# All 31 taps of the second mixer stage's convolution in four 64x64 tiles of TensorE

## What is computed

```python
def conformer_conv(a, b, w_dw, b_dw, ln_g, ln_b):
    u = a * jax.nn.sigmoid(b)
    y = lax.conv_general_dilated(          # causal, depthwise, 31 taps
        u, w_dw[:, None, :], window_strides=(1,), padding=[(CONV_KERNEL - 1, 0)],
        dimension_numbers=('NWC', 'WIO', 'NWC'), feature_group_count=CONV_WIDTH)
    y = layernorm(y + b_dw, ln_g, ln_b)
    return jax.nn.silu(y)

y_conv = conformer_conv(...)               # 512 channels
y_nsa = nsa_mixer(...)                     # 8 heads of 64
h = h + jnp.concatenate([y_conv, y_nsa], axis=-1) @ w_out[l]
```

## Time and profile before

| | us |
|---|---|
| median of 3 runs | 1631.72 (1630.59 to 1637.64) |
| span of the profiled execution | 1634.1 |
| TensorE busy | 1572.9 (96%) |
| VectorE busy | 1188.7 (73%) |
| ScalarE busy | 861.1 (53%) |
| GpSimd busy | 351.8 (22%) |

### The profile page before, as it was taken

The page is one execution under the profiler, slowest core; times in us unless marked ns, Lnnn a source line. Parts: engine busy times, 40 slices in busy tenths (PEclk is TensorE's granted clock), DMA queues, the critical chain, the costliest instruction groups (busy, mean ns, idle before and its releaser), DMA issues.

```text
span 1634.1 us, 31405 instructions
## 1 busy us (share of the span) xinstructions
PE 1572.9 (96%) x10490; PEld 1437.0 (88%) x10490; DVE 1188.7 (73%) x2258; ACT 861.1 (53%) x1587; POOL 351.8 (22%) x260
## 2 busy tenths in 40 slices
PE   8899998999999999999999999999999999999997
PEld 8789987999887887898999999988888999999996
DVE  3788676788756678455579678779998767776776
ACT  5564445655556643565554555554444545444544
POOL 2344332011000422122048755540000000000000
PEclk9899999999999999999999999999999999999999
DMA  7333244555564720154546644457777665555654
GB/s 268 126 103 104 91 142 155 171 162 180 188 194 126 234 76 1 42 191 142 168 150 203 201 149 145 136 184 241 241 241 227 201 183 190 182 190 183 189 186 148
DMA packets 87848, 271.15 MB, mean 166 GB/s; under 512 B 9824, under 2 KB 26336, under 8 KB 87392
## 3 DMA queue, kind: packets, MB, share of 16 engines
q1 hardware_dynamic: 65088, 237.01, 45.2%
q10 hardware_dynamic: 22688, 33.16, 6.2%
HBM read 258.60 MB, written 11.53 MB: 165 GB/s over the span
## 4 chain that ended last, share of the span: by engine, by line
PE 80%; DVE 11%; ACT 4%; issue 2%; POOL 1%; ACTq 1%; DMA 0%; DVEq 0%; POOLq 0%
PE ps_chunk L488 42%; PE ps_misc L488 21%; PE ps_misc L295 7%; PE ps_chunk L295 4%; PE ps_misc L2457 4%; DVE ffn_arena L1584 1%; DVE w_lo L428 1%; ACT w_hi L421 1%; PE ps_misc L798 1%; DVE mixers_arena L2257 1%; DVE mixers_arena L2258 1%; DVE mixers_arena L2254 1%; PE ps_chunk L495 1%; POOL w_lo L428 1%; DVE mixers_arena L2253 1%
## 5 line engine op out<-in xcount | busy, mean ns | idle before, releaser
L421 ACT ACTIVATE w_hi<-raw 128x512 fp32r<-128x512 f32 (+1 forms) x900 | 548.5, 626 | 495.2 <-PE ps_chunk L488 292.0
L428 DVE TENSOR_TENSOR w_lo<-raw,w_hi 128x512 fp32r<-128x512 f32 x671 | 490.1, 745 | 269.1 <-ACT w_hi L421 259.4
L488 PE MATMUL ps_chunk<-x_hi,w_hi 128*128 128x256 f32 x1792 | 520.0, 290 | 13.6 <-DVE w_lo L428 7.3
L488 PE MATMUL ps_chunk<-x_hi,w_lo 128*128 128x256 f32 x1792 | 508.6, 284 | 0.0
L488 PE MATMUL ps_chunk<-x_lo,w_hi 128*128 128x256 f32 x1792 | 508.3, 284 | 0.0
L428 POOL TENSOR_TENSOR w_lo<-raw,w_hi 128x512 fp32r<-128x512 f32 (+2 forms) x229 | 299.8, 1323 | 539.3 <-ACT w_hi L421 476.0
L488 PEld LDWEIGHTS ps_chunk<-x_hi,w_hi 128*128 128x128 f32 x1792 | 344.8, 192 | 26.1 <-POOL w_lo L428 10.2
L488 PEld LDWEIGHTS ps_chunk<-x_hi,w_lo 128*128 128x128 f32 x1792 | 345.0, 193 | 3.2 <-issue 0.5
L488 PEld LDWEIGHTS ps_chunk<-x_lo,w_hi 128*128 128x128 f32 x1792 | 344.8, 192 | 0.0
L488 PE MATMUL ps_misc<-w_hi,hid_hi 128*128 128x512 f32 x520 | 203.5, 391 | 2.1 <-DVE hid_lo L2536 1.4
L488 PE MATMUL ps_misc<-w_hi,hid_lo 128*128 128x512 f32 x520 | 203.1, 391 | 0.0
(11 more groups left out here) (342 smaller groups left out, 1795.4 us busy)
## 6 DMA issues: line engine op xcount, KB each, us to landing
raw<-in_stream SPq DMA_DIRECT2D x452, 512.0 KB, 3.6
early_rows<-row ACTq DMA_DIRECT2D x64, 128.0 KB, 1.7
row<-early_rows ACTq DMA_DIRECT2D x62, 128.0 KB, 3.2
memory_kv<-mixers_arena ACTq DMA_DIRECT2D x4, 512.0 KB, 5.2
mixers_arena<-in_cmp_w ACTq DMA_DIRECT2D x1, 2048.0 KB, 7.7
mixers_arena<-memory_kv ACTq DMA_DIRECT2D x4, 512.0 KB, 6.3
mixers_arena<-in_consts ACTq DMA_DIRECT2D x1, 1729.0 KB, 7.9
row<-in_rows ACTq DMA_DIRECT2D x3, 512.0 KB, 6.6
```

What stands on the lines that cost most here:

```text
L421: e.activation(w_hi[q % 2][:, s], raw[q][:, s], ACT.Copy).then_inc(made, 1)
L428: e.tensor_tensor(w_lo[q % 2][:, s], raw[q][:, s], w_hi[q % 2][:, s].bitcast(F32), ALU.subtract).then_inc(made, 1)
L488: last = e.matmul(o, stationary[a], moving[b], start=start and i == 0, stop=stop and i == 2, skip_group_check=True)
```

## The change

All 31 taps become products. The 128x128 diagonal of a channel tile holds two 64x64 diagonals, and the other two quarters of the array stand idle; now two channel tiles are worked on at once. For each tap and pair of tiles there are four 64x64 products: rows 0 to 63 and 64 to 127 of the first tile, summed in the same half of PSUM's partitions, and both halves of the second, summed in the other half (`rows ^ swap`). The row half chooses the bank. The diagonals are built by GpSimd in four parts of 8, 8, 8 and 7 taps per pair, with a folded identity `eye`. The taps strand, its sums in ps_chunk[0] and the four adds of L1865 are gone; instead VectorE moves each tile out of PSUM in two halves of 64 partitions, with the bias. The order string is another one: the letters t are gone and some letters c stand elsewhere.

```diff
--- before.py
+++ after.py
@@ -42,7 +42,7 @@
 NF = D_FF // P
 
 CONV_K, CONV_T = 31, 4
-CONV_PE = 20
+CONV_PART = 8
 NSA_H, NSA_G, NSA_D = 8, 2, 64
 CMP_B, CMP_S = 32, 16
 N_CMP = (T - CMP_B) // CMP_S + 1
@@ -73,9 +73,8 @@
 LAST_QUARTER_LAST = ((0, 0), (0, 1), (1, 0), (1, 1), (0, 2), (1, 2), (0, 3), (1, 3))
 
 MIXERS_2_ORDER = ("ddqddddddkddqqddddddddddddddkdddddddddkdddddddqddddddqdddddqqddkddqdqkkkkddqdkdkdddkkccddkdddddddkkk"
-                  "ddccttddkdkkqtqdkdddqqkcctttccttkkctttktctttkqqcttkkqtcccttqtttttttqqttkktctttttctttkttttqtttckttqkq"
-                  "tttttttttttttttckccctccttcccctqcckqckcckqccqkccqckckqckcccqqccqkqkccqccccckqccccqkcqckqkqdddqqkkdddd"
-                  "dddddddddddddddddddddddddddddddddddddddddckqt")
+                  "ddccddkdkkqqdkdddqqkcccckkckckqqckkqcccqqqkkcckqckqkqckcccccccccqcckqckcckqccqkccqckckqckcccqqccqkqk"
+                  "ccqccccckqccccqkcqckqkqdddqqkkdddddddddddddddddddddddddddddddddddddddddddddckq")
 
 STREAM = {}
 _at = 0
@@ -1812,9 +1811,9 @@
                 return have_2, have_cmp
 
             keys, queries = nsa(Z2, first, causal, seen, seen_add, inv, pos_raw, cmpw1, cmpw2, begin, x_parts)
-            conv, taps = conv_module(Z2, first, x_parts)
+            conv = conv_module(Z2, first, x_parts)
             weave(MIXERS_2_ORDER, dense=(0, 4, dense_chunks()), conv=(2, 2, conv), keys=(4, 2, keys()),
-                  queries=(6, 2, queries()), taps=(0, 2, taps))
+                  queries=(6, 2, queries()))
             return added_by["w_out_2"]
 
         def conv_module(Z2, first, x_parts):
@@ -1823,24 +1822,31 @@
             pad = CONV_K - 1
             U = cut(CONV_T, T + pad)
             Y = cut(CONV_T, T)
-            half = CONV_PE // 2
-            diagonals = [cut(half, P), cut(half, P)]
+            part_of_taps, side = [range(j, min(j + CONV_PART, CONV_K)) for j in range(0, CONV_K, CONV_PART)], P // 2
+            block = [slice(0, side), slice(side, P)]
+            diagonals = [cut(2, CONV_PART, side), cut(2, CONV_PART, side)]
+            eye = cut(side)
             tiles = lambda n: Z2[:, n, :].rearrange("p (k t) -> p k t", t=T)
             taps = col[:, COLS["conv_dw_w_2"][0]:COLS["conv_dw_w_2"][0] + CONV_K * CONV_T].rearrange(
                 "p (j k) -> p k j", k=CONV_T)
-            made, summed = [], [None] * CONV_T
-            sums_at = ps_chunk[0][:, :].rearrange("p (k t) -> p k t", t=T)
+            made = []
 
             def taps_by_pe():
                 used_up = [None, None]
 
-                def diagonal_taps(k, part):
-                    D_part, lo = diagonals[part], half * part
+                jobs = [(pair, part) for pair in range(CONV_T // 2) for part in part_of_taps]
+
+                def diagonal_taps(n):
+                    pair, part = jobs[n]
+                    count = len(part)
+                    each = taps[:, 2 * pair:2 * pair + 2, part[0]:part[0] + count]
                     return pool.do(lambda e: e.tensor_tensor(
-                        D_part, ident.unsqueeze(1).broadcast_to([P, half, P]),
-                        taps[:, k, lo:lo + half].unsqueeze(2).broadcast_to([P, half, P]), ALU.mult), used_up[part])
+                        diagonals[n % 2][:, :, 0:count, :],
+                        eye.unsqueeze(1).unsqueeze(1).broadcast_to([P, 2, count, side]),
+                        each.unsqueeze(3).broadcast_to([P, 2, count, side]), ALU.mult), used_up[n % 2])
                 yield from evacuated(first)
-                m = [diagonal_taps(0, 0), diagonal_taps(0, 1)]
+                pool.do(lambda e: e.tensor_tensor(eye, ident[:, 0:side], ident[:, side:P], ALU.add))
+                m = [diagonal_taps(0), diagonal_taps(1)]
                 dve.do(lambda e: e.memset(U[:, :, 0:pad], 0.0))
                 yield
                 for b, ready in enumerate((half_evacuated, evacuated)):
@@ -1848,49 +1854,33 @@
                     made.append(dve.do(lambda e, s=slice(2 * b, 2 * b + 2): e.tensor_tensor(
                         U[:, s, pad:pad + T], tiles(3)[:, s, :], tiles(4)[:, s, :], ALU.mult)))
                     yield
-                for k in range(CONV_T):
-                    at, ps, free = banks.take()
-                    for part in range(2):
-                        for some in range(0, half, 2):
-                            for j in range(half * part + some, half * part + some + 2):
-                                used_up[part] = pe.do(mm(ps[:, 0:T], diagonals[part][:, j - half * part, :],
-                                                         U[:, k, j:j + T], j == 0, j == CONV_PE - 1),
-                                                      m[part], made[k // 2], *free)
+                for n, (pair, part) in enumerate(jobs):
+                    if part[0] == 0:
+                        at, ps, free = banks.take(2)
+                    for j in part:
+                        for swap in range(2):
+                            for rows in range(2):
+                                used_up[n % 2] = pe.do(mm(
+                                    ps[block[rows ^ swap], rows * CW:rows * CW + T],
+                                    diagonals[n % 2][block[rows], swap, j - part[0], :],
+                                    U[block[rows], 2 * pair + swap, j:j + T], j == 0, j == CONV_K - 1),
+                                    m[n % 2], made[1], *free)
+                        if j % 3 != 2:
                             yield
-                        if k + 1 < CONV_T:
-                            m[part] = diagonal_taps(k + 1, part)
-                    yield
-                    while summed[k] is None:
-                        yield "early"
-                    v = dve.do(lambda e, k=k, ps=ps: e.scalar_tensor_tensor(
-                        out=Y[:, k, :], in0=ps[:, 0:T], scalar=c("conv_dw_b_2", k), in1=Y[:, k, :], op0=ALU.add,
-                        op1=ALU.add), used_up[1], summed[k])
-                    banks.release(at, 1, v)
+                    if n + 2 < len(jobs):
+                        m[n % 2] = diagonal_taps(n + 2)
+                    if j < CONV_K - 1:
+                        continue
+                    for k in (2 * pair, 2 * pair + 1):
+                        yield
+                        for rows in range(2):
+                            to, own = block[rows], block[rows ^ (k % 2)]
+                            v = dve.do(lambda e, k=k, to=to, own=own, rows=rows, ps=ps: e.tensor_scalar(
+                                Y[to, k, :], ps[own, rows * CW:rows * CW + T], c("conv_dw_b_2", k)[to], None, ALU.add),
+                                used_up[n % 2], own=False)
+                    banks.release(at, 2, v)
                 yield
                 yield from layer_norm(v)
-
-            def taps_by_dve():
-                for j in range(CONV_PE, CONV_K):
-                    for k in range(CONV_T):
-                        yield
-                        while len(made) <= k // 2:
-                            yield "early"
-                        tap, src = taps[:, k, j:j + 1], U[:, k, j:j + T]
-                        if j == CONV_PE:
-                            sums = dve.do(lambda e, k=k, tap=tap, src=src: e.tensor_scalar(
-                                sums_at[:, k, :], src, tap, None, ALU.mult), made[k // 2], own=False)
-                        else:
-                            to = Y if j == CONV_K - 1 else sums_at
-                            sums = dve.do(lambda e, k=k, tap=tap, src=src, to=to: e.scalar_tensor_tensor(
-                                out=to[:, k, :], in0=src, scalar=tap, in1=sums_at[:, k, :], op0=ALU.mult,
-                                op1=ALU.add), before[k], own=False)
-                        before[k] = sums
-                        if j == CONV_K - 1:
-                            summed[k] = sums
-                        if k % 2:
-                            yield
-
-            before = [None] * CONV_T
 
             def layer_norm(ready):
                 YT, SQ = (xn[:, i, :].rearrange("p (t n) -> p t n", t=TT) for i in range(2))
@@ -1926,7 +1916,7 @@
                     x_parts[part] = made_x
                 yield
 
-            return taps_by_pe(), taps_by_dve()
+            return taps_by_pe()
 
         def nsa(Z2, first, causal, seen, seen_add, inv, pos_raw, cmpw1, cmpw2, begin, x_parts):
```

## The result

| | before | after |
|---|---|---|
| median, us | 1631.54 (1630.59 to 1637.64, 4 runs) | 1658.40 (1652.41 to 1664.10, 4 runs) |
| ratio | | 1.0158 [1.0139, 1.0178] |
| span of the profiled execution, us | 1634.1 | 1650.5 (its time: 1652.41) |

The change costs 26.9 us, where 13.7 were forecast. Slower was right and the range held the time, but it lies above the likeliest case's own range (1637 to 1650), between it and rival (a), so the time alone doesn't tell which case came about. The four runs of after lie in two pairs: 1652.41 and 1653.64 at a mean granted clock of 0.984 and 0.983, 1663.16 and 1664.10 at 0.978 and 0.976.

What follows compares the result with a forecast made beforehand. TensorE's order in the second mixer stage, not VectorE's load, was taken as the bound. +9.7 us up to W and +4 for the clock made +13.7 on 1634.1, 1647.8; less 2.4 to the median, 1645 us; range 1637 to 1670.

Steps and rivals of the forecast that it cites:

- rival (a): Convolution products: only row halves run side by side, or the sequencer can't keep up; 0.89 us a group, 1669 us; chance 0.25.
- Taps, evacuations, diagonals: VectorE loses 21.3 us of taps and gains 8 evacuations of 0.48 us; GpSimd's diagonals take 1.9 us each, costed at nothing.
- The group: Four 64x64 convolution products on TensorE run side by side, 0.44 us a group, 27.5 us for 62 groups.
- (c): Convolution products: nothing runs side by side, 62 x 1.33 = +82 us, 1725 us; chance 0.04.
- (b): Convolution products: milder form of rival (a), eight records cost 0.5 us a group, +3.3, 1649 us; chance 0.12.
- Up to 628 us: Second mixer stage's first part: 31 groups replace 80 records, so the transposes of 627.50 come at 624.2, -3.3 us.
- The wait at the second pair: Second pair's first group waits for tile 1's last evacuation, issued on VectorE behind a softmax front: +3.7 us.
- rival (e): Evacuations are cheap and the wait at the second pair vanishes: 4 us off the forecast, inside its range; no separate chance.
- The tail: Stage end: layer norm's second turn falls behind the attention's last products; W begins 13.1 us after them; net +9.7 us.
- rival (d): Not slower: layer norm's second turn is still issued ahead of the attention's last products, 1629 to 1633 us; chance 0.09.
- The clock: TensorE's new gaps bring two to three half-clock stretches of 1.7 us each: +4 us, from none to four (6.8).
- my walk: Step-by-step timing of the second mixer stage to the last softmax, whose transposes come at 663.3, -2.4 us in all.

Runs made afterwards that it cites:

- large products: The changed kernel with one 128x128 product in place of each group of four 64x64 products, convolution not computed in full: 1656.99 us, ratio 1.0170.
- The two letters: The changed kernel with two more letters c in the order string, putting the layer norm's second turn ahead of the attention's last products: 1637.03 us, ratio 1.0031.
- the filled kernel: The changed kernel with unread identity products put into its four TensorE gaps (17, 8, 17 and 25 of them): 1652.90 us, ratio 1.0115.
- the first filling of the mended kernel: The changed kernel with two more c, four convolution banks and identity products in short waits, in a bank first needing evacuation: 1634.85 us, ratio 1.0019.
- the last kernel: The changed kernel with more c, four convolution banks, earlier evacuations and filling products in bank columns 384 to 511: 1627.60 us, ratio 0.9959.

## Why the prediction came out as it did

**Taps, evacuations, diagonals: right.** Single lines of after (least/median/most ns, first and last start), beside the earlier trace rows:

```profile
L1878 DVE TENSOR_SCALAR mixers_arena<-ps_chunk,col x8: 470/484/492, 622.6 to 667.2; 64x256 f32<-64x256 f32 x8
L1843 POOL TENSOR_TENSOR mixers_arena<-mixers_arena,col x8: 1713/1934/1937, 571.4 to 651.0; 128x1024 f32<-128x1024 f32 x6, 128x896 f32<-128x896 f32 x2
```

484 ns for the 0.48 us and 1.93 us for the 1.9.

**The group: right at 0.44 us.** 120 records in 6.71 us against 6.6 forecast and 13.3 in rival (a). Rivals (a) and (c) fall by this line, and (b) too: 120 records, each with its weight load, went out in 56 ns each. The Trainium skill's page "TensorE: Matmul & The Clock Gate" (Back-to-back issue gap) would have them at about 62 ns if the sequencer handled each; the trace doesn't agree, so here that bound doesn't bind. The Trainium skill's page "TensorEngine Tiling (Array Packing)" (Key Properties) has tiles that work independently, and 6.71 us against the 6.75 of large products agrees.

**Up to 628 us: right.** The transposes were put at 624.2 in before's terms; the stage began 1.6 us sooner, which makes 622.6. They came at 622.42.

**The wait at the second pair: right.** 3.90 us for 3.7, ended by the evacuation (L1878) behind the softmax front; rival (e) falls.

**The tail: right.** From the end of the attention's products (683.88) to W (697.21) it took 13.3 us, for 13.1; the gaps were 3.87 and 5.62 for 4.2 and 6.1, and root and table load stand where they were put. The two letters showed the cause; rival (d) falls. The turn's eight transposes took 1.97 us for 1.09, as the clock was low: 0.9 of the 13.3 are the clock's, and the rest of the tail was that much shorter than forecast.

**The clock: the term that was mis-sized.** "I take two to three, +4 us" priced each stretch by one row, 1.7 us for a burst of 20 records, as though a stretch ended soon after the gap that began it. They lasted 10.1, 6.7 and 13.5 us. The number, three, came out right, in part by luck: two began in gaps that the prediction had named, of its other two gaps the one at the layer norm's first turn (1.73 us here) began none and the last lay within a stretch, and the third stretch began behind softmax waits under 1 us, which it had put at nothing. In the profiled execution the price was:
- From the second pair's first group to the transposes behind the layer norm's first turn: 630.34 to 668.22, 37.9 us. In the filled kernel, with the clock at 1.00 throughout, the same way is 631.44 to 664.13, 32.7 us. So 5.2 us are the clock's. By my walk, less the 1.6, the transposes were due at 661.7, 6.5 us sooner; the other 1.3 us are my own sum's. Of these 0.65 are the wait ahead of the transposes at 654.02, which is in the filled kernel too: TensorE waits there for the multiply of a softmax, as the burst ahead had become shorter, and the walk left that out. The rest wasn't followed up.
- The tail: +0.2 on the forecast.
- W's first products at half level, 697.2 to 701.1: 1.9 us.

6.5 + 0.2 + 1.9 is 8.6 us where 4 stood. With the 9.7 of the walk and the tail that makes 18.3 us; less the 1.6 us by which the stage began sooner it is 16.7, and the spans differ by 16.4. The clock's own part is 5.2, 0.9 in the tail and 1.9, together 8.0 us.

**From that execution to the median.** The other 10.5 us are in the choice of executions. Before's was a slow one: with the 1.9 us that lie around the span (1652.41 less 1650.5, of after) its time was 1636.0, 4.5 above the median of 1631.54. The prediction set the span of 1634.1 against a median of times and so took 2.4 for 4.4; this changed nothing in the forecast, since the 1.9 would have stood on the other side too, and median plus 13.7 is 1645 either way. After's was the quickest of four, 6.0 below its median. In half of after's runs the clock's loss seems to be 10.6 us larger still. The term should have been about 8 us and, in every other run, 19.

What the prediction lacked was the question of what stands behind each gap. Behind the gap at 628 come softmaxes with waits of 0.9 and 0.7 us between short products; behind that at the layer norm's first turn come 128 thin products; only behind those of the tail comes dense work. The prediction had the earlier trace rows as its only look at this, a stretch of 3.30 us, and there the work after the gap was denser. That the density is what set the lengths is argued and not shown. What the level needs to rise again is open: in the trace it rose some 4 us after W began, and it stayed low through 33 us of products of 64 columns.

## What to carry to other kernels

When a strand gets more or fewer steps, count its resumptions against the order written by hand: two letters short cost 21 of the 27 us. When tiles are summed in larger groups, ask which banks the next group takes and what stands ahead of the evacuation in its engine's queue. And price a new TensorE gap not by its length but by the work that stands behind it, at the lower clock, for as long as traces of the same kernel show a stretch to last (here 3.4 to 47.6 us); then take several runs, since the clock doesn't fall in the same gap each time.

## What was unexpected of the hardware

- **A level that stays low under full load.** TensorE was busy for 33.22 of 34.0 us at a granted clock of 0.50, with 128x64 products and transposes; 104 such products cost 22.29 us instead of 11.72. The Trainium skill, "TensorE: Matmul & The Clock Gate" (What's actually happening), has the clock follow how busy TensorE has recently been; in this kernel busy in the profile's sense wasn't enough.
- **Falls without a large gap.** The clock fell behind a gap of 2.07 us in one execution, and in the softmaxes of after behind waits of 0.65 and 0.94; in the kernel with two more c the products behind a gap of 1.66 us took their full-clock 7.26, and in the first filling of the mended kernel so did those behind a gap of 2.07. No gap alone foretells it.
- **Two halves of the columns and two halves of the rows at once** cost nothing over one product of the whole array, in float32: 6.71 against 6.75 us for 15.
- **A product that begins a sum seems to disturb a running sum in other columns of its bank.** In the last kernel the filling wrote columns 384 to 511 and the sum stood in 0 to 255, and the sum still came out other. That is inferred from the outputs and no trace row shows it. The Trainium skill's page "PSUM — Partial Sum Buffer" (The four PSUM rules) says that such a product clears the marks of what has been written over the whole bank, which agrees.
